# Prompt heads 2 to 7: inverse key norms reach the 128 partitions by DMA from SBUF instead of by a one-row matmul

## What is computed

```python
def mla_keys(c, kr, w_uk, g_kn):
    k_nope = jnp.einsum('...tr,rhd->...thd', c, w_uk)
    k_rope = jnp.broadcast_to(kr[..., None, :], k_nope.shape[:-1] + (ROPE_DIM,)).astype(k_nope.dtype)
    return rmsnorm(jnp.concatenate([k_nope, k_rope], axis=-1), g_kn)

# per block of 128 queries, 8 heads of 128 + 64 dimensions
s = jnp.einsum('bqhd,bkhd->bhqk', qi, k) * ATTN_SCALE
p = jax.nn.softmax(jnp.where(mask, s, -jnp.inf), axis=-1)
return jnp.einsum('bhqk,bkhd->bqhd', p, v)
```

## Time and profile before

| | us |
|---|---|
| median of 3 runs | 3083.93 |
| lowest, highest | 3083.2, 3086.99 |
| the profiled execution | 3089.08 |
| its span in the trace | 3087.2 |
| mean granted TensorE clock | 0.985 |

### The profile page before, as it was taken

How to read it: one execution, slowest core, us unless ns; L and a number is a source line. 1 busy time by engine, 2 the same in 40 slices (tenths; PEclk the granted TensorE clock), 3 DMA queues, 4 the chain that set the end, 5 groups by cost and what they waited for, 6 DMA issues and landing times.

```text
span 3087.2 us, 69054 instructions
## 1 busy us (share of the span) xinstructions
PE 2974.6 (96%) x28799; PEld 2859.7 (93%) x28799; DVE 2105.6 (68%) x2673; ACT 1355.6 (44%) x2418; POOL 720.0 (23%) x557
## 2 busy tenths in 40 slices
PE   8999999999999999999999999999899998999999
PEld 8999997589999989999999999999888887999999
DVE  6977866656666663879777887864356555478976
ACT  4433434455555542344344443434445544334432
POOL 1322210410000002123221232430145453212321
PEclk9999999999999998999999999999999999999999
DMA  3233222111111201222232322312100001223222
GB/s 117 94 98 92 86 66 73 34 39 35 36 44 50 69 19 69 71 94 89 89 94 71 96 92 86 101 57 76 50 11 11 18 18 41 82 72 94 90 89 86
DMA packets 78973, 208.21 MB, mean 67 GB/s; under 512 B 25505, under 2 KB 42274, under 8 KB 63714
## 3 DMA queue, kind: packets, MB, share of 16 engines
q1 hardware_dynamic: 78690, 204.16, 20.9%
HBM read 198.63 MB, written 5.49 MB: 66 GB/s over the span
## 4 chain that ended last, share of the span: by engine, by line
PE 85%; DVE 8%; ACT 4%; issue 2%; POOL 1%; DMA 0%; DVEq 0%; POOLq 0%; ACTq 0%; SPq 0%
PE PS L469 25%; PE PS L285 22%; PE PS L1589 11%; PE PS L2479 6%; PE PS L2187 5%; PE PS L642 5%; PE PS L1570 1%; PE PS L1616 1%; DVE RKK L2914 1%; DVE WL L269 1%; PE PS L2167 1%; DVE DOWN L771 1%; DVE WL L435 1%; PE PS L1213 1%; PE PS L1214 1%
## 5 line engine op out<-in xcount | busy, mean ns | idle before, releaser
L408 POOL TENSOR_TENSOR WLF<-RAW 128x512 f32<-128x512 f32 x72 | 93.9, 1305 | 982.7 <-PE PS L285 657.2
L264 ACT ACTIVATE WH<-RAW 128x1536 fp32r<-128x1536 f32 (+3 forms) x112 | 171.3, 1530 | 324.5 <-PE PS L285 196.2
L269 DVE TENSOR_TENSOR WL<-RAW,WH 128x1536 fp32r<-128x1536 f32 (+3 forms) x113 | 218.0, 1929 | 118.8 <-ACT WH L264 118.8
L1589 PE MATMUL PS<-UKMH,CTH 128*128 128x384 f32 (+1 forms) x768 | 269.6, 351 | 0.8 <-POOL RQL L1532 0.8
L469 PE MATMUL PS<-XH,WH 128*128 128x288 f32 x864 | 256.0, 296 | 8.3 <-DVE M L510 8.3
L469 PE MATMUL PS<-XH,WL 128*128 128x288 f32 x864 | 256.3, 297 | 0.0
L469 PE MATMUL PS<-XL,WH 128*128 128x288 f32 x864 | 255.8, 296 | 0.0
L1663 DVE TENSOR_REDUCE SS<-SQ 128x4 f32<-128x512 f32 x256 | 173.5, 685 | 120.7 <-ACT SQ L1648 118.7
L1589 PE MATMUL PS<-UKMH,CTL 128*128 128x384 f32 (+1 forms) x768 | 253.1, 330 | 0.0
L1648 ACT ACTIVATE SQ<-PS 128x384 f32<-128x384 f32 (+1 forms) x384 | 172.2, 455 | 133.2 <-PE PS L1589 133.2
L285 PE MATMUL PS<-HH,WH 128*128 128x288 f32 x1056 | 225.6, 295 | 1.2 <-DVE WL L269 1.2
(11 more groups left out here) (636 smaller groups left out, 9050.9 us busy)
## 6 DMA issues: line engine op xcount, KB each, us to landing
RAW<-in_w SPq DMA_DIRECT2D x113, 1024.0 KB, 4.9
RAW<-in_w SPq DMA_DIRECT2D x48, 768.0 KB, 5.0
ROWS<-in_cache_c SPq DMA_DIRECT2D x128, 128.0 KB, 2.0
RAW<-in_w SPq DMA_DIRECT2D x16, 512.0 KB, 4.4
ROWS<-in_cache_kr SPq DMA_DIRECT2D x128, 32.0 KB, 1.8
RAW<-in_w SPq DMA_DIRECT2D x8, 384.0 KB, 3.3
X<-in_x SPq DMA_DIRECT2D x4, 576.0 KB, 7.7
out_y<-X SPq DMA_DIRECT2D x8, 288.0 KB, 2.3
```

What stands on the lines that cost most here:

```text
L264: act.activation(WH[n % 2][:, 0:cols], RAW[n % 2][:, 0:cols], ACT.Copy).then_inc(rounded, 1)
L269: dve.tensor_tensor(WL[n % 2][:, 0:cols], RAW[n % 2][:, 0:cols], WH[n % 2][:, 0:cols].bitcast(F32), ALU.subtract).then_inc(item_split, 1)
L1589: mm = pe.matmul(out[:, 0:c1 - c0], c[u][:, x], w, start=t == 0, stop=t == 5)
```

## The change

The inverse norms of heads 0 and 1 are spread by matmul as before. For heads 2 to 7 SyncE issues one DMA each, which reads the head's row of 512 numbers from its one partition of `RSK` and writes it to all 128 partitions of that head's part of `SQK`, whose squares are used up by then. Heads 2 and 3 are issued when `k_rs` is 1, heads 4 to 7 when it is 2, all ahead of the page loads. Each group has a semaphore, and VectorE waits for its full count (2 and 4 transfers of 16) before the first key multiplication that needs one of them. For these heads the multiplications take their second input from SBUF instead of from PSUM bank 7, and TensorE's loop has no `wide_keys`.

```diff
@@ heads_sp
         sp.dma_start(PAGES_SB[0:1, :], a["pages"].rearrange("o n -> o n")).then_inc(pages_in, 16)
+        for h in range(BY_MATMUL, H):
+            sp.wait_ge(k_rs, h // 4 + 1)
+            i = h % 4
+            sp.dma_start(SPREAD[:, h, :], RSK[32 * i:32 * i + 1, h // 4, :].unsqueeze(1).to_broadcast([1, P, SEQ])).then_inc(k_spread[h // 4], 16)
         first_rows_sp(sp)
+
+    BY_MATMUL = 2
+    SPREAD = SQK[:, :, 0:SEQ]
@@ heads_pe
             scores(h, ORDER[3:4])
-            if h + 1 < H:
-                if h + 1 == 4:
-                    pe.wait_ge(k_rs, 2)
-                wide_keys(h + 1)
             outputs(h - 1)
@@ heads_dve, keys(h)
-            dve.wait_ge(k_wide, h + 1)
-            if h >= 2:
+            if h < BY_MATMUL:
+                dve.wait_ge(k_wide, h + 1)
+                wide = bank(7)
+            else:
+                dve.wait_ge(k_spread[h // 4], 16 * (4 - BY_MATMUL if h < 4 else 4))
                 dve.wait_ge(s_mm, 4 * (h - 1))
-            dve.tensor_tensor(KS[h % 2][:], KRAW[:, h, 0:SEQ], bank(7), ALU.mult).then_inc(k_ok, 1)
-            dve.tensor_tensor(KSR[h % 2][:].rearrange("p (h t) -> p h t", h=H), KRG, bank(7).rearrange("p (h t) -> p h t", h=H), ALU.mult).then_inc(k_ok, 1)
+                wide = SPREAD[:, h, :]
+            dve.tensor_tensor(KS[h % 2][:], KRAW[:, h, 0:SEQ], wide, ALU.mult).then_inc(k_ok, 1)
+            dve.tensor_tensor(KSR[h % 2][:].rearrange("p (h t) -> p h t", h=H), KRG, wide.rearrange("p (h t) -> p h t", h=H), ALU.mult).then_inc(k_ok, 1)
```

More of the change, by code:

```diff
@@ L948, in program @@
     k_wide = stage_sem("attention", "k_wide")
+    k_spread = [stage_sem("attention", f"k_spread_{half}") for half in ("low", "high")]
     k_ok = stage_sem("attention", "k_ok")
```

## The result

The changed kernel takes 3100.62 us, the median of 5 runs (3096.62 to 3102.6), against 3086.99 us (3083.2 to 3087.26, 5 runs) of the kernel before on the same chip. The ratio is 1.0049, 95% interval 1.0037 to 1.006, some 15 us: slower, by more than the 0.2% that can be told. The profiled execution took 3102.6 us, its span 3100.6 (before: 3089.08 and 3087.2).

What follows compares the result with a forecast made beforehand. TensorE's queue, busy 96% of the span, was taken as the bound. Stall 8.7, clock 1.7 and longer periods 1.7 summed to +12.1 us: 3101.2 from the profiled execution, 3096 from the median; range 3080 to 3103.

Steps and rivals of the forecast that it cites:

- The likeliest case: Prompt heads: spreads late by 9 us, with neighbours; +12.1 us, chance 0.51, own range 3088 to 3103.
- the stall: Before head 4's scores: TensorE starts at 586.85 in place of 578.15, 8.7 us late, waiting for the last spread.
- the longer periods: Heads 5, 6 and 7 run at a period of 9.4 us, 0.57 over 8.83 each, 1.7 us together.
- The six spreads removed are worth 3.2 us, not 6.3: Heads 2 to 7: GpSimd's loop lets the period fall from 8.83 to 8.29 only, so 3.2 us are gained.
- Two inputs in SBUF hold GpSimd: Key multiplications beside GpSimd's scalings: each engine waits for the other, adding 1.1 us to GpSimd's loop, period 9.4.
- a sign of being wrong: Key multiplications staying at 0.69 us beside GpSimd was listed among the observations that would show the prediction wrong.
- A transfer from one partition takes 9.0 us: Each 256 KB spread, at one engine's share of 29 GB/s; six in one queue end at 585.5.
- The shared count makes head 4 wait for head 7's transfer: Heads 4 to 7 share one semaphore at full count, so head 4's keys, due at 575.92, wait to 585.5.
- An issue holds SyncE 0.38 us … queue cost: nothing: SyncE's spread issues: four end by 543, before the page loads start at 549.73, at no queue cost.
- The clock costs 1.7 once, at most double: After the wait before head 4's scores: TensorE's slow granted clock loses 1.7 us, at most double.
- The rest of the program costs nothing: Outside the prompt heads: no cost was counted; the stage after 620 was to cover the delayed page loads.

Runs made afterwards that it cites:

- e1: Changed kernel without its six transfers and their waits; heads 2 to 7 multiply by head 1's norms in PSUM bank 7; 3086.09 us, ratio 0.9999.
- e5: Against e4, VectorE's two key multiplications of the next head moved ahead of the last block's mask; 3086.81 us, ratio 1.0.
- e2: Against e1, the second input of the key multiplications of heads 2 to 7 lies in SBUF, still without transfers; 3089.93 us, ratio 1.0024.
- e7: Against e4, the same 24 transfers of 64 KB, but each reads a single source partition again; 3102.26 us (one run).
- e4: Changed kernel with each spread as four transfers of 64 KB, each from 32 source partitions; 3092.46 us, ratio 1.0023.
- e3: Changed kernel with a semaphore for each of the six transfers, so each head waits for its own only; 3091.33 us, ratio 1.0023.
- e8: Changed kernel, narrow transfers and shared count kept, with the key multiplications moved forward as in e5; 3099.31 us (one run).

## Why the prediction came out right, and which steps did not

The likeliest case happened, by its mechanism and near its size: +15 us by the ratio, +12.1 predicted; 3102.6 for the profiled execution, 3101.2 predicted; the median 3100.62 lies within the range, 4.6 above the point. That the whole came so near is in part luck. In the stage I had 12.1 and the profile shows 9.9: the stall was 2.6 us shorter than reckoned and the longer periods cost 1.0 less, and a second fall of the clock gave 1.5 back. The other 3.5 arose outside the stage, where I had counted nothing. Step by step:

- **The six spreads removed are worth 3.2 us, not 6.3.** Right in size (e1: 3.35), but for a wrong reason. I put ScalarE's loop at 8.1 and GpSimd's at 8.29 and so expected TensorE in front of the transposes. e1 shows ScalarE's loop at 8.28, and TensorE waiting for it. My 8.1 ended with the first copy. In e1 the copy ends 8.14 us behind the start of the outputs (573.95 to 582.09), so that part was right; left out were the 0.14 us from there to the next outputs. The kernel before shows the same at its last head, where no spread stands in front of the outputs. TensorE's timeline:

```profile
610.51 2.40 PE L1232 MATMUL PS<-PT,VS 128*128 128x512 f32 x8 [0.45 <-ACT PT L1335]
```

These start 8.3 us behind the outputs of 602.21, and wait for ScalarE's copy. GpSimd's loop, 8.29 in my sum, is 8.37 where it sets the pace (e5).
- **Two inputs in SBUF hold GpSimd.** Right that it exists: e1 and e2 differ in nothing else. Wrong in two points. I expected two holds of 1.1 us together, a period of 9.4; it is one of 0.87, all in the first scaling, and a period of 9.15. And I expected each engine to hold the other, with multiplications above 1 us; they keep 0.66 and 0.68, which I had named as a sign of being wrong. GpSimd's scaling of 567.79 takes 0.61 us when it isn't held, and it ends at 569.26, so, if it then took its own time, it ran from 568.65: it waited through both multiplications, which VectorE issues back to back. In the earlier trace rows GpSimd got in between two VectorE instructions and held the second; here it did not.
- **The Trainium skill's rule,** SBUF — State Buffer, "Who interferes with whom": the engine that has issued first keeps the shared ports for a whole instruction, and the other is blocked. The trace agrees with who is held: `KS` starts at 567.61, GpSimd at 567.79, and 1.47 us stand against 0.61. That both multiplications pass before GpSimd gets its turn is more than the rule says.
- **A transfer from one partition takes 9.0 us.** Right in size, but it is no constant. The mean is 8.57, the last lands at 582.90 instead of 585.5, and so the stall is 6.1 us instead of 8.7. The pace in the steady parts is 9.6 us, slower than my one sixteenth of the rate of large stores, and the mean lies under 9.0 only because transfers from 96 and 0, and from 32 and 64, overlap, which I had not foreseen. By the Trainium skill's 27.2 GB/s for a port (SBUF — State Buffer, "Door 1: The DMA port swizzle") a transfer takes an estimated 9.6 us. The trace agrees for the steady parts, with 27.3 GB/s in e7. Why it was slow was argued only; e4 and e7 show it, 2.0 against 9.1 us to landing with all else alike.
- **The shared count makes head 4 wait for head 7's transfer.** Right; e3 takes just that away, and the stall is gone.
- **"An issue holds SyncE 0.38 us … queue cost: nothing."** The first half was wrong. The chain has issues of 5.49 and 9.06 us, and the last holds SyncE to 566.18, where I had it free by 543. The page loads behind them start at 573.58 instead of 549.73. What they cost in the end was indeed nothing: the first transposes of page rows (L1578; L1570 before) start at 638.05 against 627.97, 10.1 us later, as much as at the stage's end.
- **The clock costs 1.7 once, at most double.** It fell twice in the stage, 1.7 + 1.5, and the second fall makes up 1.5 of the 2.6 us that the stall was short of. Of this the changed kernel gets 1.3 back right behind the stage, where the kernel before has the longer fall.
- **The rest of the program costs nothing.** I counted nothing there, and it is the last 3.5 us. By the medians every version's whole time lies 1 to 4 us above what its stage tells: e1 gains 3.35 in the stage and nothing in all, e5 gains 2.0 and nothing. What differs is the clock. Each run's time times the share of clock not granted, averaged over the runs, is 42.7 us for the kernel before beside e1 to e4 and 45.2 beside e5, and 46.3 for e1, 47.2 for e2, 47.6 for e3, 48.6 for e4, 46.8 for e5 and 52.1 for the changed kernel. For e1, 46.3 - 42.7 = 3.6 takes back the 3.35. With this loss taken off each mean time, e1 lies 3.9 us below the kernel before and e5 1.2, and e2, e3 and e4 lie 0.7, 1.5 and 1.1 above it; their stages, less the clock in them, tell -3.35, -2.0, +2.1, +1.5 and +2.2. In the profiles most of it falls in one stretch, from 2590 to 2720 us: 8.5 us are lost there before and 15.4 in the changed kernel (granted clock 0.93 and 0.88), 13.7 in e1 and e5, 15.4 in e4, but 10.2 in e2 and e3 and 8.5 in e8. The changed kernel is 9.3 us behind when it comes and 13.4 after it. What brings a fall in the later stages, and why it comes more often although they run the same instructions, no run here settles. It stays open.

## What to carry to other kernels

Before a broadcast is moved from TensorE to a DMA, count its source partitions: it is they that set the rate, and a source of 32 rows made the same 256 KB harmless. Give each consumer its own count, or order the waits so that the first consumer doesn't wait for the last transfer. And when an operand moves from PSUM to SBUF, look at what GpSimd does at that very moment, for the operation that moved may look untouched while its neighbour pays; moving it ahead by some 3 us, out of GpSimd's way, shortened the stage by 4.2 us without the clock's falls (83.75 - 3.4 in e4, 77.86 - 1.7 in e5), more than the 3.35 that the removed matmuls can give.

## What the runs showed of the hardware

- One source partition gave 27.3 GB/s (64 KB every 2.40 us in e7), while the 16 DMA engines were busy for 85% of the time. Over the six transfers it was 30.6 GB/s (256 KB in 8.57 us), since transfers from 96 and 0 and from 32 and 64 overlapped; those from 64 and 96, or 0 and 32, didn't. 32 source partitions brought each 64 KB piece home in 2.0 us.
- SyncE is not free of its transfers. Behind a backlog of such transfers a single issue held it 5.49, 9.06 and 9.66 us, where one of a page load takes 0.38.
- Two key multiplications of 0.66 and 0.68 us with both inputs in SBUF lengthened the GpSimd scaling beside them from 0.61 to 1.47 us, without growing themselves; with one input in PSUM they had no effect.
- Versions without the stall lost 1.7, 3.4 or 5.1 us to the granted clock in a stage of 80 us, by whole falls. A difference of 2 to 4 us in one profile of this kernel is no more than one or two of these.
